# Seven-product pairs: 512-column matmuls against the high weights, three chained banks a pair, and the FFN gate scaled on GpSimd

## The reference

```python
xn = rmsnorm(h, g_pre_mix)
proj = xn @ w_in          # q, k, v of two attentions, and gate_a, gate_b
...
ya = neighbourhood_attention(qa, ka, va, rpb) @ w_branch_a
yb = gqa_attention(qb, kb, vb) @ w_branch_b
mix = (jax.nn.sigmoid(gate_a) * ya + jax.nn.sigmoid(gate_b) * yb) @ w_out
h = h + rmsnorm(mix, g_post_mix)
gu = rmsnorm(h, g_pre_ffn) @ w_ffn_in
g, u = jnp.split(gu, 2, axis=-1)
h = h + rmsnorm((jax.nn.silu(g) * u) @ w_ffn_out, g_post_ffn)
e = p_l @ w_ple
h = h + rmsnorm(jax.nn.sigmoid(h @ w_ple_gate) * e, g_ple)
```

## Time and profile before

| | |
|---|---|
| median of 3 runs | 2796.68 us (2796.5 to 2797.44) |
| span of the profiled execution, first to last instruction | 2793.8 us |
| its own time | not listed apart from its span; the median of the runs is 2.9 us above the span |
| TensorE busy | 2759.9 us, 99% |
| VectorE, ScalarE, GpSimd busy | 1677.4, 997.8, 18.3 us |
| FFN pairs | about 1298 to 2106 us, 40 of them |
| gate pairs | about 56 to 301 us, 12 of them |

### The profile page before, as it was taken

The page is one execution under the profiler, slowest core; times in us unless marked ns, Lnnn a source line. Parts: engine busy times, 40 slices in busy tenths (PEclk is TensorE's granted clock), DMA queues, the critical chain, the costliest instruction groups (busy, mean ns, idle before and its releaser), DMA issues.

```text
span 2793.8 us, 41330 instructions
## 1 busy us (share of the span) xinstructions
PE 2759.9 (99%) x16624; PEld 2465.9 (88%) x16624; DVE 1677.4 (60%) x2113; ACT 997.8 (36%) x1323; POOL 18.3 (1%) x25
## 2 busy tenths in 40 slices
PE   8999999999999999999999999999999999999997
PEld 7999888888888888878999999999998888888886
DVE  7888555555554432376888888888883233234534
ACT  7333323323334322253444444444442121113422
POOL 0000000000000000000000000000000000000000
PEclk9999999999999999999999999999999999999999
DMA  6434422222225444253433333333327352443322
GB/s 251 151 114 136 138 76 75 75 84 83 75 91 163 138 153 141 91 196 136 151 114 141 122 132 131 125 138 117 146 92 295 103 181 99 157 155 124 131 96 105
DMA packets 158298, 364.75 MB, mean 131 GB/s; under 512 B 17142, under 2 KB 51438, under 8 KB 155630
## 3 DMA queue, kind: packets, MB, share of 16 engines
q1 hardware_dynamic: 146304, 325.33, 34.1%
q10 hardware_dynamic: 11886, 37.87, 3.4%
HBM read 321.15 MB, written 42.00 MB: 130 GB/s over the span
## 4 chain that ended last, share of the span: by engine, by line
PE 87%; issue 10%; DVE 1%; ACT 1%; DMA 1%; SPq 0%; POOL 0%; DVEq 0%; POOLq 0%
PE bank L2204 10%; PE bank L2202 10%; PE bank L2203 10%; PE bank L2122 10%; PE bank L2124 10%; PE bank L2123 10%; PE bank L1948 8%; PE bank L1946 8%; PE bank L1947 8%; PE bank L1979 1%; DMA x_f<-xT 0%; DVE resid_b L1643 0%; PE bank L2271 0%; PE bank L1967 0%; ACT x_f L771 0%
## 5 line engine op out<-in xcount | busy, mean ns | idle before, releaser
L736 ACT CAST w_hi<-w_raw 128x1024 fp32r<-128x1024 f32 x290 | 292.3, 1052 | 934.6 <-PE bank L2204 522.7
L1188 DVE TENSOR_TENSOR w_lo<-w_raw,w_hi 128x1024 fp32r<-128x1024 f32 x288 | 341.0, 1222 | 454.4 <-ACT w_hi L736 454.3
L2122 PE MATMUL bank<-act_hi,w_hi 128*128 128x256 f32 x1664 | 471.2, 283 | 2.4 <-DVE act_lo L1279 1.4
L2123 PE MATMUL bank<-act_lo,w_hi 128*128 128x256 f32 x1664 | 470.9, 283 | 0.0
L2124 PE MATMUL bank<-act_hi,w_lo 128*128 128x256 f32 x1664 | 470.9, 283 | 0.0
L2122 PEld LDWEIGHTS bank<-act_hi,w_hi 128*128 128x128 f32 x1664 | 319.4, 192 | 2.9 <-DVE act_lo L1279 1.6
L2123 PEld LDWEIGHTS bank<-act_lo,w_hi 128*128 128x128 f32 x1664 | 319.5, 192 | 0.1
L2124 PEld LDWEIGHTS bank<-act_hi,w_lo 128*128 128x128 f32 x1664 | 319.5, 192 | 0.0
L1946 PE MATMUL bank<-act_hi,w_hi 128*128 128x512 f32 x752 | 299.5, 398 | 1.2 <-DVE w_lo L1188 1.2
L1947 PE MATMUL bank<-act_lo,w_hi 128*128 128x512 f32 x752 | 293.2, 390 | 0.0
L1948 PE MATMUL bank<-act_hi,w_lo 128*128 128x512 f32 x752 | 293.1, 390 | 0.0
(11 more groups left out here) (263 smaller groups left out, 5422.5 us busy)
## 6 DMA issues: line engine op xcount, KB each, us to landing
w_raw<-w_in SPq DMA_DIRECT2D x92, 512.0 KB, 4.2
w_raw<-w_ffn_out SPq DMA_DIRECT2D x88, 512.0 KB, 4.5
w_a_even<-w_ffn_in SPq DMA_DIRECT2D x80, 512.0 KB, 5.3
w_a_odd<-w_ffn_in SPq DMA_DIRECT2D x60, 512.0 KB, 4.4
hid_dram<-hid_st ACTq DMA_DIRECT2D x44, 512.0 KB, 5.2
w_raw<-w_ffn_in SPq DMA_DIRECT2D x36, 512.0 KB, 5.4
w_raw<-w_out SPq DMA_DIRECT2D x32, 512.0 KB, 4.5
w_raw<-w_ple_gate SPq DMA_DIRECT2D x32, 512.0 KB, 4.3
```

Source lines behind the costliest of these rows:

```text
L736: nc.scalar.copy(w_hi[:, 2 * par + half], w_raw[:, half]).then_inc(hi_ready, 1)
L1188: nc.vector.tensor_tensor(w_lo[:, 2 * par + half], w_raw[:, half], w_hi[:, 2 * par + half].bitcast(F32), ALU.subtract).then_inc(lo_ready, 1)
L2122: nc.tensor.matmul(out, w_hi[:, slot, k], hi, start=k == 0, stop=False)
L2123: nc.tensor.matmul(out, w_hi[:, slot, k], lo, start=False, stop=False)
```

## The change

- Each step of a product is two matmuls in place of three. The high weight block is loaded once and multiplied by high and low data together, 512 columns, into both halves of a bank; the low weight block by the high data, 256 columns, goes into the first half. So a product stands in its bank as two halves that have still to be added. `act_hi` and `act_lo` become two parts of one tile `act_both`, so that one access pattern covers both.
- Products accumulate in chains over three banks, `a`, `g`, `b`, instead of seven banks; successive pairs alternate between two sets. Bank a takes products 0 and 3, bank g 1 and 5, bank b 2, 4 and 6. Bank b does not start from zero: ScalarE first copies bank a (product 0) into it.
- ScalarE makes six copies a pair (`keep_chain`): a to b, snapshots of g and of b (twice), and the second half of a and of b. VectorE makes six additions: two of 512 columns (`add_both`), four of 256 (`combine`).
- The order inside VectorE's loop: some additions come before the low weight tile of that j (`combine_first`), others behind it (`combine_second`). In the FFN pairs the product with `up` (L1861 after) comes behind the low tile too.
- In the FFN pairs GpSimd, not VectorE, multiplies `gu` by `rstd` (`scale_gate`). ScalarE's silu still waits for that.
- TensorE waits for ScalarE's copies (`kept`) at the start of products 2, 4 and 6. The first FO unit (its first block of banks) waits for all additions but one of the last pair, as counted by the new `SUMS = 4`.

```diff
+CHAIN_BANKS = ((0, 1, 5), (2, 3, 4))
+CHAIN_OF = (0, 1, 2, 0, 2, 1, 2)
+COPIES = 6
+SUMS = 4
...
+            def scale_gate(n):
+
+                pool.wait_ge(combined, n * SUMS + (GATE_PAIRS * SUMS + 3))
+                flat = gu[:].rearrange("p a t -> p (a t)")
+                nc.gpsimd.tensor_tensor(flat, flat, rstd[:], ALU.mult).then_inc(ffn_read, 1)
...
+            def keep_chain(p, q, j, before):
+
+                a, g, b = CHAIN_BANKS[q % 2]
+                if j == 0:
+                    if before > 1:
+                        act.wait_ge(combined, p * SUMS - SUMS)
+                    nc.scalar.copy(bank[:, b], bank[:, a]).then_inc(kept, 1)
+                elif j == 1:
...
+                    nc.scalar.copy(second_kept[:].rearrange("p a t -> p (a t)"), bank[:, g]).then_inc(kept, 1)
+                elif j == 2:
...
+                    nc.scalar.copy(third_kept[:].rearrange("p a t -> p (a t)"), bank[:, b]).then_inc(kept, 1)
+                elif j == 3:
+                    nc.scalar.copy(low_half[:, 0], bank[:, a, S:]).then_inc(kept, 1)
+                elif j == 4:
+                    nc.scalar.copy(fifth_kept[:].rearrange("p a t -> p (a t)"), bank[:, b]).then_inc(kept, 1)
+                elif j == 6:
...
+                    nc.scalar.copy(low_half[:, 1], bank[:, b, S:]).then_inc(kept, 1)
...
+            def combine_first(p, q, j):
+
+                a, g, b = CHAIN_BANKS[q % 2]
+                if j == 3:
+                    dve.wait_ge(kept, p * COPIES + 4)
+                    combine(gu[:, 0], low_half[:, 0], bank[:, a, 0:S])
+                if j == 4:
+                    dve.wait_ge(kept, p * COPIES + 5)
+                    add_both(fifth_kept, second_kept[:].rearrange("p a t -> p (a t)"))
+                if j == 5:
+                    dve.wait_ge(op_done, p * PRODUCTS + 6)
+                    add_both(third_kept, bank[:, g])
+                if j == 6:
+                    dve.wait_ge(kept, p * COPIES + 6)
+                    combine(up[:, 0], low_half[:, 1], bank[:, b, 0:S])
+
+            def combine_second(p, j):
+
+                if j == 4:
+                    dve.wait_ge(halves_added, p * 2 + 1)
+                    add_halves(up[:, 1], fifth_kept)
+                if j == 5:
+                    dve.wait_ge(halves_added, p * 2 + 2)
+                    add_halves(gu[:, 1], third_kept)
...
-                    nc.tensor.matmul(out, w_hi[:, slot, k], hi, start=k == 0, stop=False)
-                    nc.tensor.matmul(out, w_hi[:, slot, k], lo, start=False, stop=False)
-                    last = nc.tensor.matmul(out, w_lo[:, slot, k], hi, start=False, stop=k == HALF - 1)
+                    both = moving(j, k)
+                    nc.tensor.matmul(out.rearrange("p (a t) -> p a t", a=2), w_hi[:, slot, k], both,
+                                     start=j < 2 and k == 0, stop=False, skip_group_check=True)
+                    last = nc.tensor.matmul(out[:, 0:S], w_lo[:, slot, k], both[:, 0], start=False,
+                                            stop=k == HALF - 1, skip_group_check=True)
...
+            def chain_free(p, j, before):
+
+                if j == 0 and before > 1:
+                    pe.wait_ge(combined, p * SUMS - (2 * SUMS - 1))
+                if j == 1 and before > 1:
+                    pe.wait_ge(combined, p * SUMS - (2 * SUMS - 3))
+                if j == 2:
+                    pe.wait_ge(kept, p * COPIES + 1)
+                if j == 4:
+                    pe.wait_ge(kept, p * COPIES + 3)
+                if j == 6:
+                    pe.wait_ge(kept, p * COPIES + 5)
...
                 if kq == 0:
                     if b < 2:
-                        pe.wait_ge(combined, (GATE_PAIRS + PAIRS) * PRODUCTS - 2 * (1 - b))
+                        pe.wait_ge(combined, (GATE_PAIRS + PAIRS) * SUMS - (1 - b))
```

More of the change, by code:

```diff
@@ L273, in build @@
         junk = at("junk", R_S + 3 * KB, [P, T])
+        fifth_kept = at("fifth_kept", R_S + 3 * KB, [P, 2, S])
+        low_half = at("low_half", R_S + 5 * KB, [P, 2, S])
         diag = at("diag", R_S + 5 * KB, [P, TT, P])
@@ L405, in build @@
         op_done = sem("op_done")
-        first_kept = sem("first_kept")
+        kept = sem("kept")
+        halves_added = sem("halves_added")
         combined = sem("combined")
@@ L537, in _ @@
             fetch_tile(N_ATT + 1, w_in, ATT_TILES + 1)
-            sp.wait_ge(combined, GATE_PAIRS * PRODUCTS)
+            sp.wait_ge(combined, GATE_PAIRS * SUMS)
             sp.wait_ge(pair_out, GATE_PAIRS)
@@ L726, in _ @@
             root(NORM_FFN_IN)
+            pool.wait_ge(rstd_ready, 2)
+            def scale_gate(n):
+                pool.wait_ge(combined, n * SUMS + (GATE_PAIRS * SUMS + 3))
+                flat = gu[:].rearrange("p a t -> p (a t)")
+                nc.gpsimd.tensor_tensor(flat, flat, rstd[:], ALU.mult).then_inc(ffn_read, 1)
+            scale_gate(0)
+            with pool.Fori(1, PAIRS) as r:
+                scale_gate(r)
             root_t(FFN, 0, TT, 2)
@@ L849, in _ @@
                     act.wait_ge(op_done, p * PRODUCTS + j + 1)
-                    if j == 0:
-                        nc.scalar.copy(first_product[:], bank[:, 0, 0:S]).then_inc(first_kept, 1)
+                    if j == 0 and p < 2:
+                        act.wait_ge(unit_read, 3 + p)
+                    keep_chain(p, p, j, p)
                     p4, j4 = p + (j + 4) // PRODUCTS, (j + 4) % PRODUCTS
@@ L1108, in seven @@
                         act.wait_ge(op_done, p * PRODUCTS + (GATE_PAIRS * PRODUCTS + j + 1))
-                        if j == 0:
-                            nc.scalar.copy(first_product[:], bank[:, 0, 0:S]).then_inc(first_kept, 1)
+                        keep_chain(p0 + (GATE_PAIRS + q), q, j, GATE_PAIRS)
                         q4, j4 = q + (j + 4) // PRODUCTS, (j + 4) % PRODUCTS
@@ L1316, in weight_sum, with add_halves, add_both @@
                 nc.vector.tensor_tensor(dst, x, y, ALU.add).then_inc(w_summed, 1)
-            def product(j):
-                return bank[:, j, 0:S]
             def combine(dst, x, y):
                 return nc.vector.tensor_tensor(dst, x, y, ALU.add).then_inc(combined, 1)
+            def add_halves(dst, both):
+                return combine(dst, both[:, 0], both[:, 1])
+            def add_both(both, other):
+                return nc.vector.tensor_tensor(both[:].rearrange("p a t -> p (a t)"), both[:].rearrange("p a t -> p (a t)"),
+                                               other, ALU.add).then_inc(halves_added, 1)
+            def combine_first(p, q, j):
[19 more added lines that the diff above has]
+                    add_halves(gu[:, 1], third_kept)
             difference(0)
@@ L1396, in _ @@
                     if j == 6:
[L1397 to L1398 removed]
+                        dve.wait_ge(combined, p * SUMS + 4)
                         rows_out(up, p, 1, -1.0).then_inc(pair_out, 1)
[L1400 to L1404 removed]
                     if p == 0 and j < 4:
@@ L2109, in moving @@
                 if j in (1, 2, 4):
-                    tile = {1: d1, 2: t2, 4: d2}[j]
-                    return tile[:, k, 0], tile[:, k, 1]
+                    return {1: d1, 2: t2, 4: d2}[j][:, k]
                 kk, ts = {0: (k, slice(0, S)), 3: (HALF + k, slice(0, S)), 5: (HALF + k, slice(S, T)),
                           6: (k, slice(S, T))}[j]
-                return act_hi[:, kk, ts], act_lo[:, kk, ts]
+                return act_both[:, :, kk, ts]
             def half_product(p, q, j, h):
```

105 lines of the change are left out of this document (36 added, 69 removed).

## The result

The changed kernel takes 2930.4 us (median of 4 runs, 2924.0 to 2933.4), the kernel before 2796.6 beside it: a ratio of 1.048 [1.046, 1.049], 134 us slower. The forecast was 2855 with a range up to 2888: the sign is right, the size is not.

What follows compares the result with a forecast made beforehand. TensorE bounds the kernel before; after, a wait for ScalarE's bank copy sets the FFN pair at 21.72 us. FFN +60.8 and -0.7, gates -7.5, FO +5 give +57.6, so 2855 us, range 2828 to 2888.

Steps and rivals of the forecast that it cites:

- What bounds the kernel: Before the change TensorE runs without a gap, 20.16 us an FFN pair; VectorE and ScalarE have room.
- the new wait: Before product 2 of each next FFN pair, TensorE waits 2.3 us for ScalarE's copy of bank a to b.
- The row of steps: Operations from product 5's first matmul through VectorE, ScalarE and GpSimd to the a-to-b copy; TensorE resumes at 12.3 + X us.
- X: Length of GpSimd's 128x512 multiplication in each FFN pair, taken as 1.1 us, between 0.53 and 1.73.
- no wait in the gates: Sign to look for: waits for `kept` all before product 2 of an FFN pair, none in the gate pairs.
- the clock behind the wait: TensorE's granted clock was taken to stay at 1.00 after waits; if lowered, the time would be beyond the range.
- Gates, -1.1 for -7.5: Gate pairs: 11 save 0.75 us each, the first loses 0.7, together -7.5 us.
- End of the gates, +5.2 for 0: Stretch from the gates' end to the first FFN product: no change in the forecast, 0 us.
- FO, +6.7 for +5: Turn to FO: first unit waits for the last pair's third addition behind a late low tile; +5 us, between 0 and 8.
- GpSimd and VectorE hindering each other: Rival: an operation of up to 1.22 us lies in the FFN row once more, +48, 2903 us; 6 in 100.
- The merged matmul costing what two did: Rival: the 512-column matmul saves nothing, an FFN pair takes 22.04 us, about 2876 us in all; 4 in 100.
- Copies in time: Rival: the FFN row takes 11.1 us, not 13.4, so TensorE never waits; 2767 us, faster; 8 in 100.

Runs made afterwards that it cites:

- The filled wait: Changed kernel plus ten matmuls into an unread bank before product 2 of each FFN pair but the first: 2882.2 us, ratio 1.031.
- the run with the gate addition first: Changed kernel with VectorE's last addition into `gu` moved ahead of the low tile of j = 5: 2846.2 us, ratio 1.018.
- The gates' old order: VectorE's old order, first gate copy before ScalarE's later stores, norm on VectorE, and gate-pair additions and norm products ahead of low tiles: 2777.2 us, ratio 0.994.
- VectorE's old order: Changed kernel with VectorE's FFN additions of j = 4 and 5 and the product with `up` ahead of their low tiles: 2787.6 us, ratio 0.997.
- the run with two spare additions: Changed kernel with two VectorE additions of 128x512 in unread spare tiles while GpSimd multiplies: 2952.4 us, ratio 1.055.
- ScalarE's copies in another order: Changed kernel with each FFN pair's `hid_st` copy moved behind the next pair's copy of bank a to b: 2831.3 us, ratio 1.013.

## Why the prediction was wrong

**What bounds the kernel, and the new wait: right.** The row of steps came out as laid out. With X = 1.29 the prediction has silu at 8.53 us after product 5's first matmul, `up`'s product at 11.57 and the copy at 12.86; the trace has 8.55, 11.56 and 12.81. TensorE resumes after 13.52 us, by the prediction 12.3 + 1.29 = 13.6. X itself was 0.19 us too low, worth 7 us. (By the figure for 2048 elements in the Trainium skill, GPSIMD Engine Reference, Performance versus the Vector engine, the estimate was 1.1 to 1.2 us; the trace has 1.29.) FFN pairs whose clock stays take 22.19 us, against 21.72. One sign was given wrongly: no wait in the gates, though the prediction's own working has product 2 of the first gate pair late, and it was, by 4.2 us.

**The step that failed: the clock behind the wait.** The prediction priced a wait at its own length and dismissed more with one row: "after a wait of 2.6 us, at 343 us, its stretch still shows 1.00". It named the case and gave it neither price nor chance. A wait of 2.4 us in every pair lowered the clock in 32 of 39 turns, at about 1.4 us each. With slow first matmuls in the other turns, products 2 and 3 hold 55 us more than undisturbed ones. The filled wait gives 48 of them back by itself, with the same row of steps. The other term of the sum, the wait, was 92 us where the forecast had 39 times 2.3, 90.

The row chosen as evidence was a single one, and its 1.00 was luck. The same wait of the earlier trace rows, 2.55 to 2.56 us, stands in all 14 traces. The clock stayed at 1.00 behind it in seven of them, the kernel before and the changed one among them, and fell in the seven others. So it does in the run with the gate addition first (TensorE's timeline, then the windows view with the clock at 0.59):

```profile
346.48 0.95 PE L2012 MATMUL bank<-ident_t,qkv_f 128*128 128x128 f32 x4 [2.56 <-DVE bias L1284]
```

```profile
346.00:350.00 4.00, 3.52 (x11) 2.94 (x12) 1.72 (x3) 0.59 (x1) 0.00 (x0) 0.59 0.35 122
```

In the FFN too, single waits of the same length do both: by the measure of the table, those of 1.95 to 2.5 us lowered the clock in some turns and not in others. What decides in which turns it falls stays open. Elsewhere in the changed kernel the clock fell behind the new wait of 2.7 us at 324.78 and behind those of 4.2 and 6.5 us.

**Gates, -1.1 for -7.5.** The wait of product 2 in the first pair came as forecast (65.18 against "about 66.1"), but half clock behind it was not forecast: the pair takes 26.37 us, 2.95 more than before, where +0.7 was expected. And the other pairs save 0.38 us and not 0.75, since the product took 2.83 us in this stretch.

**End of the gates, +5.2 for 0.** The prediction didn't look past the gates. SyncE waits for the last gate output, which now stands behind low tiles that wait for transfers. TensorE waits 2.7 us for the third attention unit's weights, where it waited 1.2 before, and has half clock behind it. The gates' old order took that back: 997.7 us, a wait of 2.0 and no half clock.

**FO, +6.7 for +5: right**, with 2.8 us of half clock behind it. VectorE's old order removed it (1.0).

**Rivals.** GpSimd and VectorE hindering each other: the argument against it held, all 40 operations of the changed kernel take 1.28 to 1.30 us. But the edit that shortens the row starts it, 2.36 us in place of 1.29. (By the Trainium skill, SBUF — State Buffer, Who interferes with whom, a VectorE instruction with two SBUF inputs and a GpSimd instruction that reads SBUF contend, and the one that issues first has the shared ports for its whole instruction while the other blocks; both timelines of the run with two spare additions agree, 1.67 and 1.78 us.) The merged matmul costing what two did: wrong, products take 2.77 to 2.83 us against 2.88. Copies in time: wrong here. The 2777 us of the best run need VectorE's queue reordered in FFN and gates, ScalarE's in the first gate pair, and the norm back on VectorE, which takes that part of the change away.

## What to carry to other kernels

Price a wait of TensorE with what its clock does behind it, and ask how often it recurs: here waits of 2.4 us a pair cost 3.8. When a copy out of or into a bank becomes a condition of the next matmul, lay out the other engines' queues up to it, and put the short operations of that row ahead of the long tiles that are not yet due; that was worth 143 us here, and the faster matmul 17. Before GpSimd takes over a step, look at what VectorE runs beside it after the next edit as well, not only now.

## What the runs showed of the hardware

- The same merged product takes 2.77 us in some stretches and 2.83 in others, with the same code: the gates took 19.41 us a pair in the run with ScalarE's copies in another order, and 19.79 in the changed kernel. In the traces one pace holds over many pairs and changes at a wait. Over 52 pairs it is 20 us; kernels with merged matmuls also scatter by 4 to 12 us where the one before scatters by 3. The three-matmul product had one pace, 2.88. The cause stays open.
- A wait of only 0.2 us makes the product behind it 0.1 us longer (2.92 for 2.83, or 2.88 for 2.77, in VectorE's old order).
- ScalarE copies 512 columns from bank to bank in 0.577 us (52 copies), as fast as from a bank to SBUF (0.587).
- GpSimd multiplies 128x512 by 128x512 in 1.291 us (40 operations of the changed kernel), VectorE in 0.69 (40 of the run with the norm back on it).
